# The end of the mixers in a two-layer block: norms by a logarithm, gate units behind the retention, operands split one tile at a time

## The reference, cut to what matters

```
o_da  = rmsnorm(diff_attention(q, k, v, lam), da_subln_g[l]) * (1 - lam_init)   # 4 heads of 128
o_ret = rmsnorm(retention(rq, rk, rv), ret_norm_g[l])                           # 4 heads of 64
o_ret = o_ret * silu(r_g)
o_sc  = sc_b * causal_dwconv(sc_c * sc_x, sc_conv_w[l], sc_conv_b[l])
gates = sigmoid(gate_pre + b_gate[l])                    # gate_pre is a part of h @ w_in
y = gates[0] * (o_da @ w_branch_da) + gates[1] * (o_ret @ w_branch_ret) + gates[2] * (o_sc @ w_branch_sc)
x = x + y @ w_out[l]
```

## Time and profile before

| what | value |
|---|---|
| median of 3 runs | 3260.49 us (3259.87 to 3262.11) |
| the profiled execution | 3259.67 us, its span 3257.9 us |
| mean granted clock of TensorE | 0.983 |
| TensorE busy | 3158.3 us, 97% of the span |
| first layer's retention | from 1791.17 us on |
| second layer's retention | from 2618.07 us on |

### The profile page before, as it was taken

One profiled execution on the slowest core, in us unless ns is written; L12 is line 12 of the kernel. 1 busy time (PEld: TensorE's weight loads), 2 busy tenths in 40 slices (PEclk: granted clock), 3 DMA queues, 4 the chain that ended last, 5 costly groups with the idle time before them and its releaser, 6 DMA issues.

```text
span 3257.9 us, 42014 instructions
## 1 busy us (share of the span) xinstructions
PE 3158.3 (97%) x17280; PEld 2502.8 (77%) x17280; DVE 1815.8 (56%) x2762; ACT 1170.7 (36%) x1833; POOL 190.5 (6%) x149
## 2 busy tenths in 40 slices
PE   9999899999999889999899999999999999999999
PEld 6788778888777678887677587788877758778887
DVE  3753453343777754343586745654647774566463
ACT  4543243232444443232353323432335342343232
POOL 1222010001000020001100000000010000010000
PEclk9999999999999889999999999999999999999999
DMA  4210022222121112222212122223232112222322
GB/s 178 79 41 20 2 90 91 91 94 101 59 78 65 65 52 91 92 102 91 87 65 78 52 91 91 91 82 108 88 113 78 65 52 91 91 91 86 102 94 75
DMA packets 41564, 264.88 MB, mean 81 GB/s; under 512 B 4601, under 2 KB 4985, under 8 KB 13981
## 3 DMA queue, kind: packets, MB, share of 16 engines
q1 hardware_dynamic: 41364, 262.18, 23.5%
q10 hardware_dynamic: 8, 0.01, 0.0%
HBM read 260.07 MB, written 3.42 MB: 81 GB/s over the span
## 4 chain that ended last, share of the span: by engine, by line
PE 77%; DVE 7%; ACT 3%; issue 2%; DVEq 0%; ACTq 0%; POOL 0%; POOLq 0%
PE psum L340 22%; PE psum L342 22%; PE psum L341 22%; PE psum L1029 2%; ACT tiles L1067 1%; DVE tiles L1091 1%; PE psum L1996 1%; PE psum L1998 1%; PE psum L1997 1%; DVE w_lo L321 1%; PE psum L1908 1%; PE psum L1038 1%; DVE tiles L1862 1%; PE psum L1916 1%; PE psum L690 1%
## 5 line engine op out<-in xcount | busy, mean ns | idle before, releaser
L340 PE MATMUL psum<-hi,w_hi 128*128 128x512 f32 x3608 | 1445.9, 401 | 18.0 <-DVE lo L590 9.1
L341 PE MATMUL psum<-lo,w_hi 128*128 128x512 f32 x3608 | 1426.8, 395 | 0.0
L342 PE MATMUL psum<-hi,w_lo 128*128 128x512 f32 x3608 | 1426.3, 395 | 0.0
L321 DVE TENSOR_TENSOR w_lo<-ring,w_hi 128x1024 fp32r<-128x1024 f32 (+1 forms) x495 | 592.8, 1199 | 417.7 <-ACT w_hi L313 417.4
L340 PEld LDWEIGHTS psum<-hi,w_hi 128*128 128x128 f32 x3608 | 678.1, 188 | 189.2 <-DVE lo L590 10.2
L313 ACT ACTIVATE w_hi<-ring 128x1024 fp32r<-128x1024 f32 (+1 forms) x495 | 505.2, 1021 | 878.3 <-PE psum L342 816.1
L341 PEld LDWEIGHTS psum<-lo,w_hi 128*128 128x128 f32 x3608 | 678.0, 188 | 168.0 <-issue 7.1
L342 PEld LDWEIGHTS psum<-hi,w_lo 128*128 128x128 f32 x3608 | 677.4, 188 | 166.2
L772 DVE SCALAR_TENSOR_TENSOR xT<-xT,psum 128x512 f32<-128x512 f32 x96 | 66.0, 687 | 223.0 <-PE psum L342 223.0
L1067 ACT ACTIVATE tiles<-tiles,small 128x256 f32<-128x256 f32 (+3 forms) x176 | 95.0, 541 | 159.5 <-DVE small L1091 159.1
L1676 DVE TENSOR_TENSOR tiles<-tiles 128x512 f32<-128x512 f32 x64 | 44.3, 692 | 174.5 <-ACT tiles L1668 174.5
(11 more groups left out here) (265 smaller groups left out, 2821.3 us busy)
## 6 DMA issues: line engine op xcount, KB each, us to landing
ring<-in_weights SPq DMA_DIRECT2D x211, 1024.0 KB, 4.8
ring<-in_weights SPq DMA_DIRECT2D x28, 704.0 KB, 4.0
ring<-in_weights SPq DMA_DIRECT2D x4, 896.0 KB, 4.4
ring<-in_weights SPq DMA_DIRECT2D x3, 832.0 KB, 4.3
xT<-in_x SPq DMA_DIRECT2D x8, 256.0 KB, 5.9
tiles<-bias_repeated SPq DMA_DIRECT2D x8, 256.0 KB, 7.3
out<-xT SPq DMA_DIRECT2D x8, 256.0 KB, 2.8
held<-in_const SPq DMA_DIRECT2D x1, 1344.0 KB, 7.8
```

Of the source, the lines that this page charges most:

```text
L321: dve.tensor_tensor(self.w_lo[:, n % AHEAD, w], self.raw(n), self.w_hi[:, n % AHEAD, w].bitcast(F32), ALU.subtract).then_inc(self.lo_ready, 1)
L340: pe.matmul(out, hi, rhs.hi(first + at), start=(at == 0), stop=False)
L341: pe.matmul(out, hi, rhs.lo(first + at), start=False, stop=False)
L342: last = pe.matmul(out, lo, rhs.hi(first + at), start=False, stop=(at == end))
```

## The change

It alters the functions `tile_norms` and `gated_branches` and the schedule in `second_block`.

One `tile_norms` now serves all six tiles, in three groups of two. Each group has three ticks: squares on ScalarE and means on TensorE; Ln of both means, then Exp with scale -0.5 of both, which is the inverse root; and the multiplications on VectorE. The square root and the reciprocal are gone. The first two groups (attention tiles) stand at ticks 0, 1, 3 and 4, 6, 8 of the retention. Of the third group (retention tiles) ScalarE's and VectorE's ticks stand behind the retention, and its two means stand inside the first gate product on TensorE, behind the second and the fourth of its eight blocks (`between`).

The tanh of the retention's gate and its first VectorE operation move into a work of their own (`norms.open`), which stands before the retention together with the four small multiplications of the gains.

The splits of the eight `src` tiles leave `gated_branches` and become a `split_work`, one tile per tick: tiles 0 and 1 at ticks 4 and 5, tiles 2, 3, 6 and 7 at ticks 9 to 12, and tiles 4 and 5 at the very end. 

```
--- before.py
+++ after.py
@@ -1824,53 +1824,73 @@
-    squared, mean_done, root, tanh_done, chain, finished = (k.sem() for _ in range(6))
-    N = len(jobs)
-    def tensor(pe, n):
-        if n < N:
-            pe.wait_ge(squared, n + 1)
-            if n >= 2:
-                pe.wait_ge(root, n - 1)
-            pe.matmul(k.bank(banks[n % 2]), k.c(jobs[n][1]), sq[n % 2], start=True, stop=True).then_inc(mean_done, 1)
-    def scalar(act, n):
-        if n < N:
-            ready(act, n)
-            if n >= 2:
-                act.wait_ge(finished, n - 1)
-            act.activation(sq[n % 2], jobs[n][0], ACT.Square).then_inc(squared, 1)
-            if jobs[n][4] is not None:
-                act.activation(th[n], jobs[n][4], ACT.Tanh, scale=0.5).then_inc(tanh_done, 1)
-        if n >= 1:
-            act.wait_ge(mean_done, n)
-            act.activation(sq[(n - 1) % 2], k.bank(banks[(n - 1) % 2]), ACT.Sqrt, bias=k.eps(1e-6)).then_inc(root, 1)
-    chains = []
-    def vector(dve, n):
-        if n == 0:
-            chains.append(Chain(dve, chain))
-            for m, (o, mean, gain, factor, gate) in enumerate(jobs):
-                if factor != 1.0:
-                    chains[0].then(dve.tensor_scalar(factors[:, m:m + 1], gain, factor, None, ALU.mult))
-        else:
+    squared, mean_done, logged, inverse, tanh_done, opened, chain, finished = (k.sem() for _ in range(8))
+    gated = [n for n, job in enumerate(jobs) if job[4] is not None]
+    def mean(pe, n):
+        pe.wait_ge(squared, n + 1)
+        if n >= 2:
+            pe.wait_ge(logged, n - 1)
+        pe.matmul(k.bank(banks[n % 2]), k.c(jobs[n][1]), sq[n % 4], start=True, stop=True).then_inc(mean_done, 1)
+    def tensor(pe, t):
+        if t % 3 == 0:
+            mean(pe, 2 * t // 3)
+            mean(pe, 2 * t // 3 + 1)
+    def scalar(act, t):
+        two = range(2 * (t // 3), 2 * (t // 3) + 2)
+        if t % 3 == 0:
+            for n in two:
+                ready(act, n)
+                if n >= 4:
+                    act.wait_ge(finished, n - 3)
+                elif n >= 2:
+                    act.wait_ge(opened, len(gated))
+                act.activation(sq[n % 4], jobs[n][0], ACT.Square).then_inc(squared, 1)
+        elif t % 3 == 1:
+            for n in two:
+                act.wait_ge(mean_done, n + 1)
+                act.activation(sq[n % 4], k.bank(banks[n % 2]), ACT.Ln, bias=k.eps(1e-6)).then_inc(logged, 1)
+            for n in two:
+                act.wait_ge(logged, n + 1)
+                act.activation(sq[n % 4], sq[n % 4], ACT.Exp, scale=-0.5).then_inc(inverse, 1)
+    chains = [None]
+    def vector(dve, t):
+        if t % 3 != 2:
+            return
+        for n in range(2 * (t // 3), 2 * (t // 3) + 2):
+            o, mean, gain, factor, gate = jobs[n]
             ch = chains[0]
-            o, mean, gain, factor, gate = jobs[n - 1]
-            rs = sq[(n - 1) % 2]
-            dve.wait_ge(root, n)
-            ch.then(dve.reciprocal(rs, rs))
-            last = dve.scalar_tensor_tensor(out=o, in0=o, scalar=gain if factor == 1.0 else factors[:, n - 1:n], in1=rs,
-                                            op0=ALU.mult, op1=ALU.mult)
+            dve.wait_ge(inverse, n + 1)
+            last = dve.scalar_tensor_tensor(out=o, in0=o, scalar=gain if factor == 1.0 else factors[:, n:n + 1],
+                                            in1=sq[n % 4], op0=ALU.mult, op1=ALU.mult)
             if gate is not None:
-                ch(last)
-                dve.wait_ge(tanh_done, n)
-                ch.then(dve.scalar_tensor_tensor(out=gate, in0=th[n - 1], scalar=1.0, in1=gate, op0=ALU.add, op1=ALU.mult))
+                ch.then(last)
+                dve.wait_ge(opened, gated.index(n) + 1)
                 last = dve.scalar_tensor_tensor(out=o, in0=gate, scalar=0.5, in1=o, op0=ALU.mult, op1=ALU.mult)
             last.then_inc(finished, 1)
-    w = Work(N + 1, tensor, scalar, vector)
-    w.finished = finished
+    def open_scalar(act, t):
+        for m, n in enumerate(gated):
+            act.activation(th[m], jobs[n][4], ACT.Tanh, scale=0.5).then_inc(tanh_done, 1)
+    def open_vector(dve, t):
+        chains[0] = Chain(dve, chain)
+        for m, (o, mean, gain, factor, gate) in enumerate(jobs):
+            if factor != 1.0:
+                chains[0].then(dve.tensor_scalar(factors[:, m:m + 1], gain, factor, None, ALU.mult))
+        for m, n in enumerate(gated):
+            dve.wait_ge(tanh_done, m + 1)
+            dve.scalar_tensor_tensor(out=jobs[n][4], in0=th[m], scalar=1.0, in1=jobs[n][4], op0=ALU.add, op1=ALU.mult).then_inc(opened, 1)
+    w = Work(3 * len(jobs) // 2, tensor, scalar, vector)
+    w.open = Work(1, scalar=open_scalar, vector=open_vector)
+    w.finished, w.mean = finished, mean
     return w
@@ -1967,12 +1987,12 @@
     return w
-def gated_branches(k, l, first, h, factor, src, src_ready, branch, out, gt, part):
-    src_hi, src_lo, scaled, tanh_done, chain, read, made = (k.sem() for _ in range(7))
+def gated_branches(k, l, first, h, factor, src_lo, branch, out, gt, part, between):
+    scaled, tanh_done, chain, read, made = (k.sem() for _ in range(5))
     ks = [range(0, 4), range(4, 6), range(6, 8)]
     def tensor(pe, t):
@@ -1982,7 +2002,7 @@
             for b in range(3):
                 if d >= 1:
                     pe.wait_ge(tanh_done, 3 * (d - 1) + b + 1)
-                k.product(pe, k.bank(2 + b), n + b, h)
+                k.product(pe, k.bank(2 + b), n + b, h, between=between if t == 0 and b == 0 else None)
             return
         if d >= 1:
             pe.wait_ge(read, 3 * d)
@@ -2004,11 +2024,7 @@
         if t % 2:
             k.split_hi(act, n + 3 + AHEAD)
             return
-        if d == 0:
-            for i in range(DT):
-                src_ready(act, i)
-                act.activation(branch.hi(i), src[i], ACT.Copy).then_inc(src_hi, 1)
-        else:
+        if d >= 1:
             act.wait_ge(read, 3 * d)
         for b in range(3):
             k.split_hi(act, n + b + AHEAD)
@@ -2023,7 +2039,6 @@
         n = first + 4 * d
         if t == 0:
             chains.append(Chain(dve, chain))
-            split_tiles_lo(dve, src, branch, src_hi, src_lo)
         ch = chains[0]
         if t % 2 == 0:
             for b in range(3):
@@ -2338,29 +2353,31 @@
         if a == 0:
             act.wait_ge(turn.copied, 2)
-    diff_norms = tile_norms(k, [(k.tile(a), "mean128", k.v("subln_g", l), 1.0 - LAM_INIT[l], None) for a in range(4)],
-                            tiles(26, 28), None, k.small[:, 44:48], (0, 1), diff_ready)
-    def ret_ready(act, a):
-        act.wait_ge(ret.copied, a + 1)
-        if a == 0:
-            act.wait_ge(diff_norms.finished, 4)
-            act.wait_ge(conv.done, 2)
-    ret_norms = tile_norms(k, [(k.tile(12 + a), "mean64", k.v("ret_g", l), 1.0, k.tile(18 + a)) for a in range(2)],
-                           tiles(26, 28), tiles(24, 26), None, (0, 1), ret_ready)
+    def norm_ready(act, a):
+        if a < 4:
+            diff_ready(act, a)
+        else:
+            act.wait_ge(ret.copied, a - 3)
+    jobs = [(k.tile(a), "mean128", k.v("subln_g", l), 1.0 - LAM_INIT[l], None) for a in range(4)]
+    jobs += [(k.tile(12 + a), "mean64", k.v("ret_g", l), 1.0, k.tile(18 + a)) for a in range(2)]
+    norms = tile_norms(k, jobs, tiles(26, 28) + tiles(40, 42), tiles(40, 42), k.small[:, 44:48], (0, 1), norm_ready)
+    last_norms = Work(9, None, norms.scalar, norms.vector)
     def src_ready(act, i):
-        if i < 4:
-            act.wait_ge(diff_norms.finished, i + 1)
-        elif i < 6:
-            act.wait_ge(ret_norms.finished, i - 3)
+        if i < 6:
+            act.wait_ge(norms.finished, i + 1)
         else:
             act.wait_ge(conv.done, i - 5)
-    gates = gated_branches(k, l, n, h, rstd, tiles(0, 4) + tiles(12, 14) + tiles(20, 22), src_ready,
-                           k.halves(28, DT), tiles(4, 12), k.tile(14, 3), tiles(17, 20))
-    schedule = ticks(turn) + behind(ret, [(conv, lambda u: 2 * u), (diff_norms, lambda u: 4 * u + 3)])
+    branch = k.halves(28, DT)
+    src_split = split_work(k, tiles(0, 4) + tiles(12, 14) + tiles(20, 22), branch, src_ready, order=[0, 1, 2, 3, 6, 7, 4, 5])
+    gates = gated_branches(k, l, n, h, rstd, src_split.out_lo, branch, tiles(4, 12), k.tile(14, 3), tiles(17, 20),
+                           lambda pe, at: norms.mean(pe, 3 + at // 2) if at in (2, 4) else None)
+    others = Work(6, norms.tensor, norms.scalar, norms.vector)
+    schedule = ticks(turn) + [(norms.open, 0)] + \
+        behind(ret, [(conv, lambda u: 2 * u), (others, lambda u: (0, 1, 3, 4, 6, 8)[u]), (src_split, lambda u: (4, 5, 9, 10, 11, 12, ret.ticks, ret.ticks)[u])])
+    schedule = schedule[:-2] + [(last_norms, t) for t in (6, 7, 8)] + schedule[-2:]
     n += 4 * DT
     gated = n
@@ -2375,7 +2392,7 @@
     n += DT
     gate_ticks, splits = ticks(gates), ticks(split)
```

(2 more changed lines are left out.)

## The result

| what | before | after |
|---|---|---|
| median | 3260.53 us (4 runs) | 3243.47 us (4 runs, 3242.87 to 3248.51) |
| ratio | | 0.9949 (0.9938 to 0.9961) |
| the profiled execution | 3259.67 us | 3248.51 us |
| mean granted clock | 0.983 | 0.982 |

The forecast was 3243, in a range of 3240 to 3251. The same kernel, run again beside the experiments, gave 3241.63 us (five runs, 3241.05 to 3242.99; ratio 0.9942, 0.9929 to 0.9954, against 3260.98 us). The profiled execution is the slowest of the first four: the other three took 3242.87 to 3243.52 us. It shows what its two layers do differently.

The account below looks back on a forecast made before the run. TensorE, busy 97% of the span, was taken to lose 10.2 us per layer behind the retention. Less a 1.65 us opening wait, 8.5 per layer, 17.0 in both, gave 3243 us from 3259.67; range 3240 to 3251.

Parts of the forecast that it names:

- What bounds the kernel: TensorE between retention and branch product: 29.10 us for 18.90 us of work, so 10.2 us per layer lost.
- The tail: Retention's end to branch product: two means of 1.05 us each and 16.80 us of gate products, 18.90 us without waits.
- The late chain: ScalarE's and VectorE's last norms and fourth unit's split behind the retention: done at R + 13.7, 5 us to spare.
- R: The end of the last retention matmul on TensorE, from which the times behind the retention are counted.
- The opening: Retention's start: TensorE waits 1.65 us for the first square; a tanh table load adds 0 or 1.28, taken as 0.
- The second group: Third mean, in the retention: TensorE has 4.9 us of work, ScalarE's chain 4.0; no wait, 0.9 us to spare.
- VectorE in the retention: VectorE loses four reciprocals there (13.4 us) and gains 3.9 us of subtractions, 0.61 us each.
- The sum: 10.20 less 1.65 is 8.5 us per layer, 17.0 us for both layers, giving 3243 us.
- The clock: The 1.65 us opening wait brings no fall, so nothing is counted; a fall would cost 1.7 us per layer.
- rival B: ScalarE late in the retention; TensorE waits at third mean or, with clock falling, opening: 3249 or 3253 us; chance 0.20.
- C: No gain: the time saved comes back as another wait behind the stage, such as for weights: 3260 us; chance 0.06.
- D: Slower: TensorE waits for ScalarE's whole chain three times a layer, 8.3 us longer per layer, 3277 us; chance 0.06.

Follow-up runs that it names:

- run 4: Changed kernel with the gate's two tanh and their VectorE part moved from before the retention to its tick 12, first norm groups one tick later: 3240.75 us.
- run 2: Changed kernel with square root on ScalarE and reciprocal on VectorE in place of Ln and Exp, the new order alone: 3282.37 us (ratio 1.0068).
- run 1: The changed kernel once more, unaltered: 3241.63 us, five runs between 3241.05 and 3242.99.
- run 6: Changed kernel with all eight splits in one block behind the last norms, in place of one tile per tick: 3243.69 us.
- run 8: Changed kernel with two unread tanh of a constant tile added on ScalarE ahead of the gate's two, lengthening the opening wait: 3255.38 us, eleven runs.

## Why the prediction was right, and where it was off

*What bounds the kernel.* Right. The 10.2 us per layer between the retention and the branch product were the whole of what was to be had; the branch product now follows the gates at once. What is won by this is 10.6 us per layer (29.10 to 18.52); the retention, with its opening wait, takes 1.25 us back (26.41 to 27.66).

*The tail.* 18.90 us were forecast and 18.52 came. The term that was off is the mean inside a product: from the first product's start at 1818.39 to 1836.99 there are 18.60 us for 16.80 us of products and two means, so 0.9 us for a mean where 1.05 was taken. The late chain was forecast to end at R + 13.7 and ended at R + 13.5 (1831.98 - 1818.47).

*The opening.* 1.65 us forecast, 1.52 measured, on the square, as said. Between the ends 0 and 1.28 us for the tanh's load it was 0. The Trainium skill ("ScalarE: Activation LUTs", Table sets) says that tanh and exp share a set; the row of L1880, which has no load in front of it behind the attention's Exp, agrees.

*The second group.* No wait, as forecast. 0.9 us of slack was computed, and 1.0 is there: the third square is ready 0.6 us behind its start at 1798.86, and TensorE comes at 1800.47. Run 4 shows how thin that is: with the opening gone and the same four ticks between the groups, TensorE comes 0.58 us too early.

*VectorE in the retention.* The prediction took four reciprocals (13.4 us) out of it and put 3.9 us of subtractions in. The retention of the kernel before held only three, 10.0 us; the fourth starts behind it, at 1819.24. The six subtractions take 4.7 us (0.79 each, not 0.61), the norms' four multiplications (L1870) 3.9 where two took 1.5, and the gate's part adds 1.3. VectorE's busy time there went from 21.86 to 20.83 us, so 1.0 us less and not 9.5. It cost nothing, since TensorE waited for VectorE nowhere, but the room was much smaller than the prediction says; run 2 fills it.

*The sum.* 17.0 us forecast, 17.1 between the medians of the first call and 19.3 in the second. A layer with its clock up gives 9.3 us, not 8.5, so 18.6 us for two: 0.4 us more come from the tail (10.6, not 10.2), and 0.4 from the retention, which grew by 1.25 and not by 1.65. The near-perfect agreement of 3243 with 3243.47 is therefore in part luck: the saving was put too low by 1.6 us, and the clock was left out. For the two profiles all is accounted for: 3257.9 - 3240.3 = 17.6 us of span in run 1 are 18.6 in the layers and 0.35 at the start, less 1.5 for the fall at L590, which the profile before doesn't have. Whether that fall is also why the first call's medians are only 17.1 apart is not shown, as those executions have no trace.

*The clock.* This is the step that was wrong, though the time came out within the range. "1.65 us is below all that fell, so I count nothing; a fall would cost 1.7 us per layer." The rows that it went by were a wait of 2.10 us between dense products, after which the clock stayed up, and one of 3.36 us. Here a wait of 1.52 us was enough, in three openings of ten. And the wait of 2.10 us was no safe ground: the same wait was followed by the lower clock in eleven of the twenty places where the profiles have it, so one trace in which a wait leaves the clock up doesn't show that it always does. The price of 1.7 us was right in two of the three openings (1.65 in run 6, 1.8 in run 2) and not in the third (6.46), where the clock stayed down for 13.7 us in place of 3.4. The slowest execution, 3248.51, lies inside the range of 3240 to 3251, whose upper part was meant for rival B (a table load and the clock, 3249).

*The rivals.* Of B's two places the opening waited, but without a table load; the third mean waited only in run 4. C didn't come: from the first layer's branch product to the second layer's first score it is 771.3 us after the change and 771.4 before, so nothing behind the stage took the gain back. D put TensorE behind ScalarE's chain in each of three groups; it stood there only at the first, for 1.52 us. The Trainium skill ("ScalarE: Activation LUTs", What ACT_TABLE_LOAD costs) adds a drain of 1.38 us to the load at every switch to a different set. It isn't in these rows: the load starts 0.02 us behind the squares (1819.00 + 1.14 to 1820.16) and Ln 0.01 us behind its load (1820.16 + 1.28 to 1821.45). With two drains ahead of it the third mean would have waited, and it doesn't.

## What to carry to other kernels

Where a chain of short steps on two other engines stands between two long runs of TensorE, put products that don't need its result in front of it, and look first whether the chain's parts fit beside the work that they are moved to: here the order without the cheaper method cost 21.4 us, and the method without the order gave 4.4. Work that is moved ahead of a stage stands in the queue in front of the first thing that TensorE waits for, so place it behind that. Don't price a wait of TensorE by its length alone, since the clock may fall with it: the same opening wait was followed by no fall in seven of ten cases, by 1.65 or 1.8 us in two and by 6.46 us in one. Look at a wait in several traces before calling it harmless.

## What the runs showed of the hardware

These are all from the ten profiles of this case. A wait of TensorE of 1.52 us at the retention's opening was followed by the lower clock in three of ten cases, one of 2.56 us in two of two. A wait of 2.08 to 2.10 us between dense products (L590) was followed by it in eleven of twenty, none of them in the kernel before. The matmuls around it and the wait itself are the same in the twenty, so neither the wait's length nor what stands around it in the program decides alone; what does was not tried.

How long the clock stayed down differed too, with TensorE busy without a gap. Behind the wait between dense products it was some 3.4 us each time. In the retention it was 3.4 us in runs 2 and 6, 13.7 in the changed kernel, 13.6 and 17.0 in run 8. With further waits in the retention (run 2) it was 30.7 us in either layer, to the retention's end.
